# The 64-row sample tile of three large products, computed as two column halves of the array side by side

## The reference, cut to what matters

```python
D_MODEL = 1024; SEQ = 1024; DEC_BATCH = 8; DEC_SEQ = 8; DEPTH = 2; D_FF = 2816
def hybrid_layer(x, l, ...):
    mixed, new = token_mixers(rmsnorm(x, p['norm_mix'][l]), ...)
    x = x + mixed
    hf = rmsnorm(x, p['norm_ffn'][l])
    x = x + (jax.nn.silu(hf @ p['w_gate'][l]) * (hf @ p['w_up'][l])) @ p['w_down'][l]
    return x, new
def token_mixers(h, l, ...):
    proj = h @ p['w_in'][l]                                    # input projection
    ...                                                        # three head groups
    mixed = jnp.concatenate([y_a, y_b, y_c], -1) @ p['w_out'][l]   # output projection
```

## Time and profile before

| what | value |
|---|---|
| median of 3 runs | 6780.59 us (6777.11 to 6792.77) |
| the profiled execution: span, first to last instruction | 6785.8 us |
| PE busy | 5678.2 us, 84% |
| PEld, DVE, ACT, POOL busy | 51%, 43%, 22%, 11% |
| mean granted TensorE clock | 0.868 |

### The profile page before, as it was taken

How to read it: one execution, slowest core, us unless ns; L and a number is a source line. 1 busy time by engine, 2 the same in 40 slices (tenths; PEclk the granted TensorE clock), 3 DMA queues, 4 the chain that set the end, 5 groups by cost and what they waited for, 6 DMA issues and landing times. The chain is left out here.

```text
span 6785.8 us, 62816 instructions
## 1 busy us (share of the span) xinstructions
PE 5678.2 (84%) x22554; PEld 3493.1 (51%) x22554; DVE 2916.9 (43%) x6698; ACT 1480.2 (22%) x2844; POOL 741.8 (11%) x776
## 2 busy tenths in 40 slices
PE   6999686465789899999989996863757879999997
PEld 4544464344567456654455444642545664666543
DVE  2257564367644233330032566533775442334200
ACT  2210122046243111100033102221553331110000
POOL 2400175000000000000033003740000000000000
PEclk9999688575789999999989996975757889999998
DMA  4222233120000231121132313322000013211122
GB/s 148 87 93 81 72 109 95 27 67 15 11 19 5 111 131 50 57 69 59 50 117 82 107 68 89 110 71 68 26 14 19 11 61 120 76 57 50 58 74 93
DMA packets 358055, 462.83 MB, mean 68 GB/s; under 512 B 70258, under 2 KB 261172, under 8 KB 357332
## 3 DMA queue, kind: packets, MB, share of 16 engines
q1 hardware_dynamic: 320932, 358.82, 16.4%
q0 software_dynamic: 36864, 100.71, 4.8%
HBM read 347.87 MB, written 121.69 MB: 69 GB/s over the span
## 5 line engine op out<-in xcount | busy, mean ns | idle before, releaser
L396 PE MATMUL pp<-w_in,nT 128*128 128x512 f32 x2016 | 909.3, 597 | 0.0
L3309 PE MATMUL pm<-w_down,hT 128*128 128x512 f32 x1584 | 685.5, 596 | 24.3 <-DMA hT<-scratch_hT 24.3
L3236 PE MATMUL pg<-nT,wgu 128*128 128x364 f32 (+1 forms) x2112 | 670.1, 471 | 16.5 <-DMA wgu<-in_w_up 16.5
L3236 PE MATMUL pu<-nT,wgu 128*128 128x364 f32 (+1 forms) x2112 | 665.1, 468 | 0.0
L396 PEld LDWEIGHTS pp<-w_in,nT 128*128 128x128 f32 x2016 | 375.6, 191 | 428.0 <-issue 427.3
L3236 PEld LDWEIGHTS pg<-nT,wgu 128*128 128x128 f32 x2112 | 403.7, 191 | 261.1 <-issue 21.1
L3236 PEld LDWEIGHTS pu<-nT,wgu 128*128 128x128 f32 x2112 | 401.4, 190 | 242.2
L3309 PEld LDWEIGHTS pm<-w_down,hT 128*128 128x128 f32 x1584 | 302.9, 191 | 406.4 <-issue 406.4
L2478 POOL DMA_INDIRECT k_sel<-in_cache_k,kv_idx x256 | 247.4, 966 | 985.2 <-DVE kv_idx L2622 860.1
L3261 DVE TENSOR_SCALAR sig<-exp_neg 128x364 f32<-128x364 f32 x132 | 46.1, 349 | 680.6 <-ACT exp_neg L3247 680.6
L3262 DVE RECIPROCAL exp_neg<-sig 128x364 f32<-128x364 f32 x132 | 319.4, 2419 | 4.5
(11 more groups left out here) (667 smaller groups left out, 8449.5 us busy)
## 6 DMA issues: line engine op xcount, KB each, us to landing
w_in<-in_w_in SPq DMA_DIRECT2D x14, 2048.0 KB, 9.8
scratch_hT<-hT SPq DMA_DIRECT2D x44, 576.0 KB, 2.8
hT<-scratch_hT SPq DMA_DIRECT2D x18, 1408.0 KB, 7.2
wgu<-in_w_gate SPq DMA_DIRECT2D x44, 512.0 KB, 3.9
wgu<-in_w_up SPq DMA_DIRECT2D x44, 512.0 KB, 5.2
w_down<-in_w_down SPq DMA_DIRECT2D x22, 1024.0 KB
x_all<-scratch_x SPq DMA_DIRECT2D x27, 512.0 KB, 15.6
a_tile<-scratch_pa SPq DMA_DIRECT2D x18, 516.0 KB, 4.9
```

The costliest lines, as they stand in the source:

```text
L396: ins = pe.matmul(pp[u % 2][:, 0:cw], nT[:, k, t * P:(t + 1) * P], w[:, k, 0:cw], start=(k == 0), stop=(k == KT - 1))
L3236: ins = pe.matmul(bank[:, 0:cw], wb[b][:, which, k, :], nT[:, k, c0:c0 + cw], start=(k == 0), stop=(k == KT - 1))
L3309: ins = pe.matmul(pm[b][n][:, :], h[b][:, k, :], w[:, k, n * 512:(n + 1) * 512], start=(k == 0), stop=(k == FT - 1))
```

## The change

The sample tile alone is computed differently in the three products. Its stationary operand is now only the 64 live rows, so it fills 64 columns of the array. The weight block is split in two, and each half is streamed against its own 64 columns: half `e` goes to PSUM partitions `64e` to `64e+63`. In the front a unit of 8 matmuls of 128x512 becomes 16 of 64x256; in the output projection 16 of 128x512 become 16 of 64x512, in the last product 44 become 44, with the two blocks now interleaved inside the `k` loop. ACT's eviction becomes two copies of 64x256; DVE's two additions of the sample tile take 64 partitions and both wait for the last matmul. GpSimd zeroes one buffer more, since rows 64 to 127 of it aren't written. Only the live columns of `hT` are stored, and loaded for the last tile.

```diff
@@ stage_front, POOL
+                pool.memset(pr[1][:, :], 0.0).then_inc(zeroed, 1)
@@ stage_front, PE
                     for k in range(k0, k1):
-                        ins = pe.matmul(pp[u % 2][:, 0:cw], nT[:, k, t * P:(t + 1) * P], w[:, k, 0:cw], start=(k == 0), stop=(k == KT - 1))
+                        if t == NT and c != IK:
+                            for e in range(2):
+                                ins = pe.matmul(pp[u % 2][e * NS:(e + 1) * NS, 0:256], nT[:, k, SEQ:SEQ + NS], w[:, k, e * 256:(e + 1) * 256], start=(k == 0), stop=(k == KT - 1))
+                        else:
+                            ...
@@ stage_front, ACT
+                    if t == NT and c != IK:
+                        act.wait_ge(zeroed, 3)
+                        act.activation(pr[u % PR][0:NS, 0:256], pp[u % 2][0:NS, 0:256], ACT.Copy)
+                        act.activation(pr[u % PR][0:NS, 256:512], pp[u % 2][NS:P, 0:256], ACT.Copy).then_inc(chunk_out, 1)
@@ stage_mix_out, PE
-                    for n in range(2):
+                    if t == NT:
                         for k in range(KT):
-                            ins = pe.matmul(pm[t % 2][n][:, :], yT[t % 2][:, k, :], w[:, k, n * 512:(n + 1) * 512], start=(k == 0), stop=(k == KT - 1))
-                        ins.then_inc(mixed, 1)
+                            for n in range(2):
+                                ins = pe.matmul(pm[t % 2][0][n * NS:(n + 1) * NS, :], yT[t % 2][:, k, 0:NS], w[:, k, n * 512:(n + 1) * 512], start=(k == 0), stop=(k == KT - 1))
+                        ins.then_inc(mixed, 2)
@@ ffn_up, SP and DVE
-                    sp.dma_start(sc["hT"][bass.ds(f + b, 1), :, :].rearrange("o p n -> (o p) n"), h[b][:, :]).then_inc(stored[b], 16)
+                    sp.dma_start(sc["hT"][bass.ds(f + b, 1), :, :].rearrange("o p n -> (o p) n")[:, 0:LIVE], h[b][:, 0:LIVE]).then_inc(stored[b], 16)
-                for b in range(2):
-                    dve.memset(h[b][:, LIVE:ROWS], 0.0)
@@ ffn_down, PE
+                def samples(t, b):
+                    pe.wait_ge(h_loaded[b], nth_load(t, b))
+                    for k in range(FT):
+                        for n in range(2):
+                            ins = pe.matmul(pm[b][0][n * NS:(n + 1) * NS, :], h[b][:, k, 0:NS], w[:, k, n * 512:(n + 1) * 512],
+                                            start=(k == 0), stop=(k == FT - 1))
+                    ins.then_inc(down, 2)
...
-                with pe.Fori(1, TILES - 1, 2) as i:
+                with pe.Fori(1, TILES - 3, 2) as i:
                     step(i, 1)
                     step(i + 1, 0)
+                step(TILES - 2, 1)
+                samples(TILES - 1, 0)
@@ ffn_down, DVE
+                def samples(t, b):
+                    dve.wait_ge(x_loaded[b], nth_load(t, b))
+                    dve.wait_ge(down, 2 * t + 2)
+                    for n in range(2):
+                        c = slice(n * 512, (n + 1) * 512)
+                        dve.tensor_tensor(x[b][0:NS, c], pm[b][0][n * NS:(n + 1) * NS, :], x[b][0:NS, c], ALU.add).then_inc(x_new, 1)
```

More of the change, by code:

```diff
@@ L395, in slice_of @@
                     for k in range(k0, k1):
-                        ins = pe.matmul(pp[u % 2][:, 0:cw], nT[:, k, t * P:(t + 1) * P], w[:, k, 0:cw], start=(k == 0), stop=(k == KT - 1))
+                        if t == NT and c != IK:
+                            for e in range(2):
+                                ins = pe.matmul(pp[u % 2][e * NS:(e + 1) * NS, 0:256], nT[:, k, SEQ:SEQ + NS], w[:, k, e * 256:(e + 1) * 256], start=(k == 0), stop=(k == KT - 1))
+                        else:
+                            ins = pe.matmul(pp[u % 2][:, 0:cw], nT[:, k, t * P:(t + 1) * P], w[:, k, 0:cw], start=(k == 0), stop=(k == KT - 1))
                     if k1 == KT:
@@ L510, in evict @@
                 def evict(u):
-                    c, _ = UNITS[u]
+                    c, t = UNITS[u]
                     cw = SMALL if c == IK else 512
@@ L517, in evict @@
                     act.wait_ge(chunk_done, u + 1)
-                    act.activation(pr[u % PR][:, 0:cw], pp[u % 2][:, 0:cw], ACT.Copy).then_inc(chunk_out, 1)
+                    if t == NT and c != IK:
+                        act.wait_ge(zeroed, 3)
+                        act.activation(pr[u % PR][0:NS, 0:256], pp[u % 2][0:NS, 0:256], ACT.Copy)
+                        act.activation(pr[u % PR][0:NS, 256:512], pp[u % 2][NS:P, 0:256], ACT.Copy).then_inc(chunk_out, 1)
+                    else:
+                        act.activation(pr[u % PR][:, 0:cw], pp[u % 2][:, 0:cw], ACT.Copy).then_inc(chunk_out, 1)
                 def relu(J):
@@ L624, in lay_queries @@
                 def lay_queries():
-                    dve.wait_ge(zeroed, 2)
+                    dve.wait_ge(zeroed, 3)
                     dve.wait_ge(i_loaded, 16 * (2 + 5 + 2 * IH))
@@ L3098, in _ @@
                         pe.wait_ge(x_new, 2 * t - 2)
-                    for n in range(2):
+                    if t == NT:
                         for k in range(KT):
-                            ins = pe.matmul(pm[t % 2][n][:, :], yT[t % 2][:, k, :], w[:, k, n * 512:(n + 1) * 512], start=(k == 0), stop=(k == KT - 1))
-                        ins.then_inc(mixed, 1)
+                            for n in range(2):
+                                ins = pe.matmul(pm[t % 2][0][n * NS:(n + 1) * NS, :], yT[t % 2][:, k, 0:NS], w[:, k, n * 512:(n + 1) * 512], start=(k == 0), stop=(k == KT - 1))
+                        ins.then_inc(mixed, 2)
+                    else:
+                        for n in range(2):
+                            for k in range(KT):
+                                ins = pe.matmul(pm[t % 2][n][:, :], yT[t % 2][:, k, :], w[:, k, n * 512:(n + 1) * 512], start=(k == 0), stop=(k == KT - 1))
+                            ins.then_inc(mixed, 1)
                     if t >= 1:
@@ L3157, in add @@
                         c = slice(n * 512, (n + 1) * 512)
-                        dve.tensor_tensor(x[:, t, c], pm[t % 2][n][:, :], x[:, t, c], ALU.add).then_inc(x_new, 1)
+                        if t == NT:
+                            dve.tensor_tensor(x[0:NS, t, c], pm[t % 2][0][n * NS:(n + 1) * NS, :], x[0:NS, t, c], ALU.add).then_inc(x_new, 1)
+                        else:
+                            dve.tensor_tensor(x[:, t, c], pm[t % 2][n][:, :], x[:, t, c], ALU.add).then_inc(x_new, 1)
                 def turn_out(t):
@@ L3282, in _, with load, step @@
             def _(sp):
-                def load(t, b):
-                    sp.dma_start(h[b][:, :, :], hT[:, :, bass.ds(t * P, P)]).then_inc(h_loaded[b], 16)
+                def load(t, b, n=P):
+                    sp.dma_start(h[b][:, :, 0:n], hT[:, :, bass.ds(t * P, n)]).then_inc(h_loaded[b], 16)
                     sp.dma_start(x[b][:, :], rows_at(sc["x"], t * P)).then_inc(x_loaded[b], 16)
-                def step(t, b, more=True):
+                def step(t, b, more=P):
                     sp.wait_ge(x_new, 2 * t + 2)
@@ L3291, in step @@
                     if more:
-                        load(t + 2, b)
+                        load(t + 2, b, more)
                 load(0, 0)
@@ L3298, in _ @@
                     step(i + 1, 1)
-                step(TILES - 3, 0)
-                step(TILES - 2, 1, more=False)
-                step(TILES - 1, 0, more=False)
+                step(TILES - 3, 0, more=NS)
+                step(TILES - 2, 1, more=0)
+                step(TILES - 1, 0, more=0)
             @block.tensor
@@ L3327, in step @@
                         dve.tensor_tensor(x[b][:, c], pm[b][n][:, :], x[b][:, c], ALU.add).then_inc(x_new, 1)
+                def samples(t, b):
+                    dve.wait_ge(x_loaded[b], nth_load(t, b))
+                    dve.wait_ge(down, 2 * t + 2)
+                    for n in range(2):
+                        c = slice(n * 512, (n + 1) * 512)
+                        dve.tensor_tensor(x[b][0:NS, c], pm[b][0][n * NS:(n + 1) * NS, :], x[b][0:NS, c], ALU.add).then_inc(x_new, 1)
                 step(0, 0)
-                with dve.Fori(1, TILES - 1, 2) as i:
+                with dve.Fori(1, TILES - 3, 2) as i:
                     step(i, 1)
                     step(i + 1, 0)
+                step(TILES - 2, 1)
+                samples(TILES - 1, 0)
 def stage_mix_ffn(nc, l, io, sc, const):
```

## The result

The changed kernel takes 6708.5 us (median of 4 runs, 6705.52 to 6709.12), the kernel before on the same chip 6778.85 (4 runs, 6776.51 to 6792.77). The ratio is 0.9897, with a 95% interval from 0.9883 to 0.9911: 70 us less, anything from 60 to 79. I had forecast 83 less and 6698 us, with a range of 6688 to 6740. The direction and the mechanism came out, and the gain is 13 us smaller than the forecast. The profiled execution took 6708.37 us.

What follows compares the result with a forecast made beforehand. PE's matmul streaming was taken as the bound; front 18.5, output projection 6.2 and last product 18.2 made 42.9 us a layer, 85.8 for two. Less half of a 6 us strict-order charge: 83 us, forecasting 6698 us, range 6688 to 6740.

Steps and rivals of the forecast that it cites:

- the mechanism: In all three products two column halves stream at once, halving the sample tile's streaming time; chance 0.68.
- half overlap: Rival, all three products: one half's load waits for the other half's stream; 53 us gained, 6728 us; chance 0.13.
- none: Rival, all three products: no overlap, only two additions a stage exposed; 2.8 us more, 6783 us; chance 0.10.
- exposed loads: Rival, all three products: no overlap and weight loads exposed; 92 us more with the additions, 6873 us; chance 0.09.
- The strict-order charge: Runs of halves: PE starting records strictly in order would cost 3 us a layer, 6 in all; half was taken.
- I take zero for the switch: Changing matmul shape around a run costs nothing; upper end 0.22 us for each of 15 runs a layer, 6.6 in all.
- The four slices of unit 18: Front, units 18 and 27: eight slices fall from 1.72 to 0.86 us each, 6.9 us a layer.
- The search step: Front, units 36, 45, 54: PE waits for DVE's count, so each gains only 1.6 us, 4.8 for three.
- wrong in size alone: Front: PE's waits in the search might make the clock fall, shown by the granted clock of 420 to 715 us.
- Units 63 and 1: Front: half of each unit's full-clock work goes, 3.4 us for each unit.
- The output projection: Half of 13.7 us of streaming saved, 6.9, minus 0.7 for an exposed addition: net 6.2 us a layer.
- The last product: Half of the sample tile's streaming saved, 18.9 us, minus 0.7 for an exposed addition: net 18.2 us a layer.

Runs made afterwards that it cites:

- e6: The changed kernel with the two loops exchanged, all of one half's matmuls before the other's: 6916.66 us, ratio 0.9961 to the kernel before.
- e5: The changed kernel with 64 columns kept but everything sent through the first column half: 6948.85 us against 6946.23 for the kernel before, ratio 1.0008.
- e1: The whole changed kernel again, in more rounds: 71 us less than the kernel before, whose median was 6926.59 us.
- e2: The kernel before with only the front taken from the change: 20 us less by medians, interval 12 to 24 us.
- e10: The changed kernel unaltered, as a control on another chip: 6700 us, where the kernel before took 6776.68 us.
- e8: The changed kernel with units 18 and 27 each run whole, their four key-score pieces behind them: 6705 us; the kernel before took 6776.68 us.
- e7: The changed kernel without search steps behind units 36, 45 and 54: ratio 0.9869 to the kernel before.

## Why the prediction was right, and where its size was off

**The mechanism, right.** The halves run at once. The pair of row halves in the earlier trace rows was the right guide to column halves. The rivals fall with one row each: half overlap wanted 5.4 us a unit and 53 us in all, none 6.9, exposed loads more still; it is 3.6. In the records' starts of the kernel after, the two halves' records start 6 ns apart, and the pairs follow each other every 0.216 us for 256 columns and every 0.429 us for 512, the bare streaming time of the earlier trace rows; so neither load waits for the other half's stream. The rule of the Trainium skill (TensorE: Matmul & The Clock Gate, Part 3, "The mechanism") would have priced the half overlap if no background buffer were free; the trace shows no such wait here.

**The strict-order charge, wrong.** I took off 3 us for records started in order. The charge isn't there: both halves start together, and e6 shows PE reaching 4 records ahead.

**"I take zero for the switch" was wrong.** I went by L431's neighbours, 64-column transposes that pay nothing, and had 0.22 us from the 64-row line as the upper end. Measured it is 0.34 us a run, with the first records, on leaving, and on entering, and e5 shows it with one half alone. But it is paid only where the neighbours are full matmuls. The four slices of unit 18 give 0.51 us each and not 0.86, 2.0 us; unit 27, between the small pieces of the new keys, gives 3.4 us in its four. Together 5.4 us a layer instead of 6.9, so 2.9 us of the total are gone.

**The search step, right in kind.** I had 1.6 us for each of units 36, 45 and 54. Units 45 and 54 give 1.6 (5.50 from step to step against 7.09, idle 1.62). At unit 36 DVE first copies the last turn out of PSUM (0.42 us from 450.61) and starts its count 1.50 us after PE's step, at 451.52, where at unit 45 it starts it 0.89 us after, at 515.87; step to step is 6.11 us instead of 7.26, and 1.15 is the gain. In layer 1 the clock then fell behind PE's 1.95 us wait and unit 37 took 1.8 us more from step to step (456.13 to 465.17 is 9.04, not 7.26). So the whole search is 2.3 us shorter in layer 1 (first to last count 221.15 to 218.83) and 4.0 in layer 2, 6.3 instead of 9.6. This is the case that I had named as wrong in size alone. The clock fell in layer 1 of this kernel after and of its repetitions (e1, e2, e10), not in layer 2, where the wait is the same 1.95 us; in e8 it is the other way round. So it is not the layer that decides; what does is open.

**Units 63 and 1.** The last count to L486 is 3.2 us shorter in each layer (3.4 forecast). Unit 1 takes 5.24 us to the next line instead of 8.65 in the first pair of profiles, also 3.4. But this pair flatters it: in four of the eight old fronts of the table unit 1 took only 6.91 us, and in the eight new ones it took 4.9 to 6.0. Up to the first piece of the key scores the front takes 68.1 us in layer 1 and 66.5 in layer 2 by the means of the old form, 64.7 and 66.7 by those of the new: 3.4 and -0.2, together 3.2 instead of 6.8. This stretch scatters by 1 to 6 us between executions of the same form, so it is the least certain of the terms. What holds up the path behind unit 1 is not shown.

**The output projection** gained 6.5 us a layer, not 6.2: ACT's copy of the previous turn ended as late as the second addition, which thus cost nothing. **The last product** gained 19.0 and 17.1 us, 36.1 for 36.4: the charge of one run is nothing beside 88 records.

The front's parts as measured are, for both layers, 10.9 (slices), 6.3 (search), 6.3 and 3.2 (units 63 and 1), less 0.5 behind L486, where it got that much longer: 26.2 us, the difference of the stages. Against the forecast's 37.0 the front lacks 3.6 us at unit 1, 3.3 in the search, 2.9 in the slices, 0.5 at unit 63 and 0.5 behind it. The 3 us that I took off for an order that PE does not keep hid a part of this: without them the forecast would have been 86. That 83 came as near as it did is in part luck. The sum of all changed stages, 75 us, lies among the three timed differences, 70, 71 and 76. The two first profiled executions differ by 79, in part since the front of before was in layer 1 3 us above its mean. Whether a microsecond or two is given back in the stages that don't change can't be told: they scatter by more than that, with no sign that repeats.

## What to carry to other kernels

A stationary operand of 64 columns leaves half the array idle; two such products over the same rows, alternated record by record, take the streaming time of one, and it pays most in long runs, since every run that stands between full matmuls pays some 0.35 us for its shape. Where another engine paces PE step by step, look at what the shortened work was covering before counting it: there the gain goes into a wait. Moving the pacing step to a longer unit gets it back, if the steps do not run on into the next short unit, as they did in e7. Read the price of a shape from a row with the same kind of instruction, not from a transpose that looks like it.

## What the runs showed of the hardware that was not expected

- Independent matmuls on the two column halves start out of program order, but only 4 records (two multiplications) ahead: 4 + 4 records overlap wholly (1.02 us), 16 + 16 hardly (6.24 us instead of 3.6), and of 44 + 44 again only the last 4 of the first half.
- A run with a 64-column operand between full matmuls costs about 0.34 us beyond its streaming, with one half in use or both; between matmuls of 64x64 and 64x128 it costs nothing on top (unit 27). Eight 64-column transposes between full matmuls cost none of it either (and L436 above, whose 0.88 us to L457 is as before). One difference is in sight: such a transpose is one record, a multiplication two. Whether that is the reason is not shown.
- The clock fell to its low level once in the searches of one execution, behind the 1.95 us of idle PE at unit 36: in layer 1 in the kernel after, e1, e2 and e10, in layer 2 in e8, never in both layers, and not behind 1.62 us at units 45 and 54.
- The stage with the gathers takes some 75 and 85 us a layer more on two chips (485 to 511 us) than in the runs on the chip of e7 and in the first comparison (412 to 421), whatever the kernel.
